# First stage of a fused two-block kernel: the tiles for q, kv and index key ahead of the second head pair, and the last five tiles as one and four

## The reference

```python
xn = rmsnorm(x, norm_g)
p = xn @ w_in
p_shift, g_rwkv, q_down, kv_down, k_idx_raw, w_idx, g_attn = jnp.split(p, IN_SPLITS, axis=-1)
y_rwkv = rwkv7_branch(p_shift, g_rwkv, ...)      # 8 heads, a recurrence over the tokens
y_attn = dsa_branch(q_down, kv_down, k_idx_raw, w_idx, g_attn, ...)
#   c_q = rmsnorm(q_down), c_kv = rmsnorm(kv_down), k_idx = layernorm(k_idx_raw)
#   q_idx = c_q @ w_qidx; for each block of 128 queries: score of all earlier keys, the 256 best kept
```

## Time and profile before

| what | value |
|---|---|
| median of 3 runs | 4196.97 us |
| profiled execution | 4205.36 us, its span 4203.6 us |
| mean granted TensorE clock | 0.965 |
| PE busy | 3898.8 us, 93% of the span |
| first stage | 0 to 844 us; its second half (chunks 2 and 3) from about 410 us |
| PE waits of 485 to 845 us | 7.9 us at the stage's end, and about 25 us in smaller ones |

### The profile page before, as it was taken

The page is one execution under the profiler, slowest core; times in us unless marked ns, Lnnn a source line. Parts: engine busy times, 40 slices in busy tenths (PEclk is TensorE's granted clock), DMA queues, the critical chain, the costliest instruction groups (busy, mean ns, idle before and its releaser), DMA issues. The chain is left out here.

```text
span 4203.6 us, 76236 instructions
## 1 busy us (share of the span) xinstructions
PE 3898.8 (93%) x31096; PEld 2744.4 (65%) x31096; DVE 2701.7 (64%) x5092; ACT 2074.8 (49%) x3077; POOL 1280.9 (30%) x1016
## 2 busy tenths in 40 slices
PE   6999999999888999889798999797999999999889
PEld 5777765756666666666586878684555555555577
DVE  5656677767777787888654332445777777777443
ACT  3434597768677777866333221222333333333431
POOL 2212222322544454453110000002445444454200
PEclk9999999999999999999899999898999999999999
DMA  3334232322211212122465333663223232231343
GB/s 122 113 103 146 68 104 92 117 65 58 67 36 38 51 43 53 46 57 70 143 215 200 120 138 133 242 207 95 66 56 89 56 79 56 63 82 29 104 143 110
DMA packets 389534, 407.18 MB, mean 97 GB/s; under 512 B 115937, under 2 KB 288417, under 8 KB 388929
## 3 DMA queue, kind: packets, MB, share of 16 engines
q1 hardware_dynamic: 388096, 399.00, 32.7%
q10 hardware_dynamic: 1088, 3.32, 0.2%
HBM read 249.74 MB, written 152.47 MB: 96 GB/s over the span
## 5 line engine op out<-in xcount | busy, mean ns | idle before, releaser
L144 ACT ACTIVATE PT<-psum 128x1024 f32<-128x1024 f32 x384 | 394.3, 1027 | 667.1 <-PE psum L134 666.6
L172 DVE TENSOR_REDUCE m<-psum 128x1 f32<-128x1024 f32 x384 | 468.1, 1222 | 281.8 <-PE psum L134 281.7
L134 PE MATMUL psum<-xc,wah 128*128 128x512 f32 x1600 | 530.9, 413 | 11.2 <-DVE xc L148 5.8
L148 POOL TENSOR_TENSOR part<-PT 128x1024 f32<-128x1024 f32 x144 | 341.8, 2374 | 473.5 <-DVE all L148 379.3
L148 POOL TENSOR_TENSOR Lm<-gm,cst 64x512 f32<-64x512 f32 x192 | 258.2, 1345 | 380.3 <-PE psum L134 194.0
L134 PE MATMUL psum<-PT,V 128*64 128x512 f32 x1536 | 371.5, 605 | 0.0
L134 PEld LDWEIGHTS psum<-xc,wah 128*128 128x128 f32 x1600 | 301.7, 192 | 97.1 <-issue 22.9
L134 PE MATMUL psum<-hc,w4h 128*128 128x512 f32 x1024 | 320.1, 394 | 8.7 <-DVE w4l L148 8.7
L134 PE MATMUL psum<-xc,wal 128*128 128x512 f32 x800 | 318.0, 397 | 0.0
L145 ACT ACTIVATE bias<-score,cand,cols 128x2048 bf16<-128x2048 f32 (+4 forms) x155 | 244.5, 1578 | 78.8 <-DVE cand L155 75.0
L145 ACT ACTIVATE sgn<-score,cand,cols 128x1920 bf16<-128x1920 f32 (+4 forms) x155 | 227.9, 1470 | 58.7 <-DVE cand L155 57.4
(11 more groups left out here) (379 smaller groups left out, 8847.8 us busy)
## 6 DMA issues: line engine op xcount, KB each, us to landing
raw_a<-in_w_a SPq DMA_DIRECT2D x50, 512.0 KB, 3.7
raw_w<-in_w_in SPq DMA_DIRECT2D x32, 512.0 KB
QNh<-scr_qnh SPq DMA_DIRECT2D x48, 256.0 KB, 4.9
QRh<-scr_qrh SPq DMA_DIRECT2D x96, 128.0 KB, 4.7
QNl<-scr_qnl SPq DMA_DIRECT2D x48, 256.0 KB, 6.3
xin<-in_x SPq DMA_DIRECT2D x16, 512.0 KB
scr_AR<-AR SPq DMA_DIRECT2D x32, 256.0 KB, 2.2
scr_BK<-BK SPq DMA_DIRECT2D x32, 256.0 KB, 2.2
```

The source lines that it names most:

```text
L134: return self.e.matmul(out, a, b, start=start, stop=stop, skip_group_check=True)
L144: return self.e.activation(out, src, f, bias=bias, scale=scale)
L148: return self.e.tensor_tensor(out, a, b, op) if self.e else self.vector(out)
L172: return self.e.tensor_reduce(out, a, AX, op, negate=negate) if self.e else self.vector(a)
```

## The change

The table of groups is now one for each half (both alike). Tiles 0 to 3 move from third to second place, ahead of 13, 14, 15, 12; the last five tiles, before in groups (24, 5) and (6, 7, 8), are now (24) and (5, 6, 7, 8), the order within them being the same. `load_a` names which load serves which tile and half; the buffers, the waits and the work are otherwise as before.

```diff
-        groups_a = [(4, 9, 10, 11), (13, 14, 15, 12), (0, 1, 2, 3), (17, 18, 19, 16), (21, 22, 23, 20), (24, 5), (6, 7, 8)]
-        tiles_a = [t for group in groups_a for t in group]
+        groups_a = ([(4, 9, 10, 11), (0, 1, 2, 3), (13, 14, 15, 12), (17, 18, 19, 16), (21, 22, 23, 20), (24,), (5, 6, 7, 8)],
+                    [(4, 9, 10, 11), (0, 1, 2, 3), (13, 14, 15, 12), (17, 18, 19, 16), (21, 22, 23, 20), (24,), (5, 6, 7, 8)])
+        tiles_a = [t for groups in groups_a for group in groups for t in group]
+        load_a = {(t, n // NW): n for n, t in enumerate(tiles_a)}
...
-                    q.dma(raw_a[s % 2][:, :, :], A["w_a"][tiles_a[s % NW]]).then_inc(*d_wa[s % 2].up(s))
+                    q.dma(raw_a[s % 2][:, :, :], A["w_a"][tiles_a[s]]).then_inc(*d_wa[s % 2].up(s))
...
-                    s = NW * (c // 2) + tiles_a.index(t)
+                    s = load_a[(t, c // 2)]
...
-                        q.wait_ge(a_pe, "p", *last_a[(tiles_a[(s - 4) % NW], (s - 4) // NW)])
+                        q.wait_ge(a_pe, "p", *last_a[(tiles_a[s - 4], (s - 4) // NW)])
```

More of the change, by code:

```diff
@@ L662, in program @@
         for half_ in range(2):
-            for gi, group in enumerate(groups_a):
+            for gi, group in enumerate(groups_a[half_]):
                 for c in (2 * half_, 2 * half_ + 1):
@@ L670, in program @@
                         nxt = c + 1
-                    elif gi == len(groups_a) - 1 and c == 1:
+                    elif gi == len(groups_a[half_]) - 1 and c == 1:
                         nxt = 2
@@ L952, in act_a @@
                     if c > 1 and i % 4 == 0:
-                        q.wait_ge(a_pe, "p", tiles_a[-1], c - 2)
+                        q.wait_ge(a_pe, "p", tiles_a[NW - 1], c - 2)
                     for j in range(2):
```

## The result

The changed kernel takes 4189.91 us (median of 20 runs), the kernel before in the same session 4195.81 us: a ratio of 0.9986, 95% interval 0.9979 to 0.9992. That is 5.9 us faster, where 9.5 were forecast; 4189.91 lies in the forecast's own range (4180 to 4193). One of the 20 executions of the kernel before was in a slower state (4478 us) and is left out of the ratio; without it the median before is 4195.60.

A forecast was written before the change was run, and what follows sets the result against it. PE, busy for 93% of the span, was taken as the bound. 0 - 7.5 - 7 + 4 + 1 = -9.5 us on the profiled 4205.4, so 4187.5 against 4197.0, written 4187; forecast 4180 to 4193 (0.45), wider range 4172 to 4209.

The forecast's parts named there:

- First half, passage: First half and passage to chunk 2: PE already full, transposes wait as before; gain 0, first half between -1 and +2 us.
- The backlog: 540 to 663 us, ACT's queue: copies of tiles 0 to 3 come sooner; -7.5 of 10.5 us lost, bounds -10.5 and 0.
- The chain: Chunk 3's norms to the gate sharing `rs`: 17.2 - 2.4 (DVE) - 3.2 (PE cover) = 11.6, taken as 10; -7 us.
- Later in the half: Tiles 16.3 to 8.2: DVE gets 11 us more work, six gates in a row share `rs`; +4 us, bounds 0 and 20.
- The stage's end: Last search result issued about 4 us behind the last tile, the 2.5 MB nearly through; +1 us, bounds 0 and +4.
- My measure of loss by windows: Second half: a window's loss is idle time plus busy time times (1 - clock); 29.7 us from 485 to 695.
- Nothing that can be told: Rival: chain as long as before, or late waits give back the backlog's gain; 4196 us, chance 0.27.
- Slower: Rival: six gates in a row hold PE if gate 24.2 lies 20 us or more behind its tile; 4210, chance 0.15.
- Better: Rival: chain hides under two tiles (-12), backlog gone (-10), nothing late; 4175 us, chance 0.13.
- That the end groups do nothing: Rival: for the last five tiles the change doesn't do what it says; contained in the forecast, no chance of its own.
- Table loads: ACT: 72 instead of 74 in the program, 1283 ns each; 2.6 us of ACT time, inside the backlog and chain terms.

The follow-up runs named there:

- e3: The kernel before with the new table of groups in the first half only: ratio to the kernel before 0.9991 (0.9982 to 1.0).
- e8: Against the kernel before: tiles 0 to 3 fourth in the second half, old end groups, tiles 0 to 3 second in the first: ratio 1.0003.
- e6: The changed kernel with a buffer of their own for the norms (a free half of `sq`): ratio to the kernel before 0.9977.
- e11: The changed kernel with the gates behind chunk 3's norms writing their tanh into two buffers by turns: ratio to the kernel before 0.9979.
- e2: The kernel before with only the last five tiles regrouped as (24) and (5, 6, 7, 8), both halves: ratio 0.9998.
- e9: e7 with the weight subtractions from load 37 on moved from DVE to POOL: ratio to the kernel before 1.0026.
- e7: Against the kernel before: tiles 0 to 3 second in both halves, old end groups, norms with their own buffer: ratio 0.9976.

## Why the prediction was right or wrong

- **First half, passage: 0.** Right. The passage waits are 3.53 and 1.58 us against 3.53 and 1.90, the row at 491.98 has moved by 0.06 us, and e3 shows nothing.
- **The backlog, -7.5 of 10.5.** Right, and more: 0.8 us are left instead of 3. The reason was half right: e8 has such waits without the copies, so head pair 1's side work beside the searches makes them as well, and moving it helped too. How the 10 us divide between the two isn't settled.
- **The chain, -7.** The place and the mechanism (the buffer `rs`) are right, and e6 shows the latter; the size is -4.4. The failed step is "17.2 - 2.4": DVE's list is shorter by 2.4 us, but the chain isn't. From the first norm's product to the next tile it takes 621.18 - 580.55 = 40.6 us, 39.6 before. ACT and DVE don't work it off without gaps: the first reciprocal starts 7.0 us behind its product, 6.1 before, with passes of both searches in between on ACT, now at 1024 and 896 columns (before 768 and 896). With the 3.2 us more of PE's work under it, that alone would give 17.2 + 1.0 - 3.2 = 15.0 us; 12.8 were measured, and the 2.2 between I can't name.
- **Later in the half, +4.** Mechanism right, a little too small. From tile 16.3's end (711.71 before, 695.28 after, from PE's rows) to PE's last it takes 10.3 us longer; side work of some 4.7 us (`lora`, `kk`, `bt`, `bonus`, two `log`) has moved into this stretch, which leaves +5.6. e11 prices the one buffer for the gates in a row, whose waits bring the low clock (0.96 from 770 to 808), at 7.0 us.
- **The stage's end, +1.** The order was right (issue 4.0 us behind the last tile, 1.7 ahead before), and so was that the 2.5 MB are nearly through by then; the cost is 0.1. What I missed is that the search result's issue moved by only 0.6 us while PE's end moved by 6.2, so that it is now a bound of its own only 1.5 us away, so that of a larger gain of PE nearly all would have been lost there (e11).
- **The sum.** By the tiles' ends PE won 16.4 - 4.7 = 11.7 us up to tile 16.3, where I had 14.5, and gave 5.6 back, where I had 4: -6.1, and with the stage's end -6.0 instead of -9.5. My measure of loss by windows gives more: 29.7 and 7.1 behind 695 before, 27.2 after, so 9.6 us. Some 1.2 of the difference is the measure's own: the mean clock of a window counts the low clock of idle time as well (663 to 695 in five pieces gives 16.9, not 17.2; 600 to 663 loses 2.5 at the low clock, not 3.0; 596 to 622 gives 13.2, not 12.8). The other 2.3 us I can't place.
- **The rivals.** "Nothing that can be told" is excluded by the interval of 20 runs, but not by the line that the prediction drew for itself: 4189.91 is 1.3 us above its 4188.6, in the stretch that it called the same. "Slower": the mechanism is there, but its condition isn't met; gate 24.2 is multiplied 10 us behind its tile (773.05 against 762.79), not 20. It is gates 5.2 and 6.2 that come 21 and 23 us behind theirs. "Better" failed at the chain. That the end groups do nothing holds beside the other part and not alone (e2).
- **Table loads.** 31 in the second half, two less than before as forecast, 1283 ns each with 0.6 us idle ahead of all of them, as in the earlier trace rows; the drain that the Trainium skill adds ("ScalarE: Activation LUTs", section "What ACT_TABLE_LOAD costs") has no gap in these rows to stand in.

## What to carry to other kernels

A scratch buffer that two chains share couples all that wait for either, and the order in which an engine works doesn't show it: look for one whose next writer waits for another chain's last reader, and give each its own first, since this costs a few lines. Count a won microsecond only up to the next thing that ends the stage: here the last search result was issued 4 us behind PE's end, and of 7 us more won on PE 1.3 arrived. And before moving a step to an idle engine, look at what the donor does meanwhile.

## What the runs showed of the hardware

An elementwise instruction of POOL with two inputs stops one of DVE with two inputs in SBUF for its whole length: 2.60 us instead of 0.48 beside a subtraction of 2.44. DVE's two tiny instructions of a `flip` (0.21 us) and one with an input in PSUM (`bon<-psum,vx`, 0.41) keep their length beside e9's subtractions, but `lda<-tw`, with one input of 128x256, took 2.51 and 2.50 us instead of 0.29 beside two of the 13. The Trainium skill, "SBUF — State Buffer", section "🔬 SBUF: two separate sides", says that the two share one pair of ports under an exclusive lock, so that the loser blocks fully; the row agrees. The group rows of DVE from 600 to 850 us, e9 and then e7, show the sum of it in one kind:

```profile
L148 DVE TENSOR_TENSOR k<-rk,t1k 128x256 f32<-128x256 f32 x12 | 10.5, 872 | 0.0
```

```profile
L148 DVE TENSOR_TENSOR k<-rk,t1k 128x256 f32<-128x256 f32 x12 | 5.3, 444 | 0.0
```

And the landing of one 160 KB DMA took 8.7, 3.3 or 1.8 us, depending on whether it left 2.0, 7.7 or 14.6 us behind the first of 2.5 MB of loads on the same queue (the kernel before, the changed one, e11). In e8, where it left ahead of them, it took 1.8 us too.
